# A two-layer decoder trunk on one core: where the dense query and gate products stand among the state updates of the scan stage

## What is computed

```python
proj = h @ p["w_in"]
z, xbc, dt_raw, rg_x, rg_gate, q, k, v, g = split(proj, ...)
y_ssd, ssd_buf_new, ssd_h = _ssd_mixer(z, xbc, dt_raw, ssd_h0, ssd_buf, p)   # the scan
y_ret, ret_h = _retention_mixer(q, k, v, g, pos, ret_h0, p)                  # reads q, k, v, g
mix = concatenate([y_ssd, y_rg, y_ret], -1) @ p["w_out"]

# in the scan, for every sequence with its own kept state S (16 heads x 128 x 64):
y = scores @ v + (q * exp(acum)) @ S       # the kept state is read
S_new = chunk_decay * S + chunk_state      # then scaled and added to
```

## Time and profile before

| | |
|---|---|
| median of 3 runs | 1962.3 us (1961.86 to 1969.98) |
| profiled execution, its own time | 1966.48 us |
| its span | 1964.6 us |
| TensorE matmul busy | 1555.6 us, 79% |
| VectorE busy | 752.6 us, 38% |
| ScalarE busy | 347.8 us, 18% |
| mean DMA rate | 289 GB/s |
| layers | two, the second some 939 us behind the first |

### The profile page before, as it was taken

How to read it: one execution, slowest core, us unless ns; L and a number is a source line. 1 busy time by engine, 2 the same in 40 slices (tenths; PEclk the granted TensorE clock), 3 DMA queues, 4 the chain that set the end, 5 groups by cost and what they waited for, 6 DMA issues and landing times.

```text
span 1964.6 us, 29459 instructions
## 1 busy us (share of the span) xinstructions
PE 1555.6 (79%) x11754; PEld 838.6 (43%) x11754; DVE 752.6 (38%) x1685; ACT 347.8 (18%) x773; POOL 113.6 (6%) x162
## 2 busy tenths in 40 slices
PE   5999988888767767668699998998896776676782
PEld 2764533434433334334266553343353333333441
DVE  0242655667222222122625355466732221122235
ACT  1235311112101111101123531110211111011010
POOL 3000012101000000000020001111000000000000
PEclk8999999988988888889899899998878888788896
DMA  9344335527799999999935443644649999999992
GB/s 332 130 172 176 119 107 178 205 116 286 328 429 428 428 428 429 428 428 427 354 123 195 142 150 96 187 148 180 278 190 428 427 429 429 428 428 429 428 427 85
DMA packets 93463, 567.52 MB, mean 289 GB/s; under 512 B 7062, under 2 KB 7918, under 8 KB 68035
## 3 DMA queue, kind: packets, MB, share of 16 engines
q1 hardware_dynamic: 81666, 532.05, 66.5%
q0 software_dynamic: 11712, 34.32, 6.2%
HBM read 550.53 MB, written 15.81 MB: 288 GB/s over the span
## 4 chain that ended last, share of the span: by engine, by line
PE 45%; DMA 39%; DVE 8%; ACT 2%; issue 2%; DVEq 2%; SPq 1%; PEldq 0%; ACTq 0%; PEld 0%
DMA ring<-in_exp_w_up 36%; PE ps L1453 10%; PE ps L940 8%; PE ps L965 8%; PE ps L1191 3%; PE ps L1316 2%; PE ps L866 2%; DMA ring<-in_w_out 2%; PE ps L947 2%; PE ps L1428 1%; DMA ring<-in_w_ada 1%; PE ps L808 1%; PE ps L1137 1%; PE ps L1161 1%; SPq L604 1%
## 5 line engine op out<-in xcount | busy, mean ns | idle before, releaser
L1453 PE MATMUL ps<-ring,xTb 128*32 128x256 f32 x4224 | 329.1, 480 | 239.9 <-DMA ring<-in_exp_w_up 234.3
L1453 PEld LDWEIGHTS ps<-ring,xTb 128*32 128x32 f32 x4224 | 163.4, 137 | 404.9 <-issue 360.8
L2530 DVE TENSOR_TENSOR hb<-sg,ps 128x128 f32<-128x128 f32 x66 | 25.0, 380 | 493.9 <-ACT sg L1792 493.9
L965 PE MATMUL ps<-ring,hT 128*128 128x512 f32 x384 | 182.7, 630 | 21.4 <-DVE h0s L2106 14.2
L940 PE MATMUL ps<-hT,ring 128*128 128x288 f32 x640 | 165.5, 418 | 5.9 <-ACT hT L1573 2.4
L1428 PE MATMUL ps<-sel,h_tm 128*128 128x128 f32 (+1 forms) x912 | 169.5, 314 | 0.0
L1428 PEld LDWEIGHTS ps<-sel,h_tm 128*128 128x128 f32 x912 | 129.6, 195 | 55.3 <-issue 29.7
L940 PEld LDWEIGHTS ps<-hT,ring 128*128 128x128 f32 x640 | 122.8, 195 | 44.1 <-issue 9.5
L1467 PE MATMUL ps<-ring,hTb 128*32 128x256 f32 x2112 | 130.7, 389 | 5.1 <-DVEq L2533 5.1
L965 PEld LDWEIGHTS ps<-ring,hT 128*128 128x128 f32 x384 | 74.8, 200 | 127.6 <-issue 127.1
L1792 ACT ACTIVATE sg<-ps 128x128 f32<-128x128 f32 x66 | 18.3, 277 | 597.7 <-PE ps L1453 597.7
(11 more groups left out here) (444 smaller groups left out, 1628.3 us busy)
## 6 DMA issues: line engine op xcount, KB each, us to landing
ring<-in_exp_w_gate SPq DMA_DIRECT2D x66, 2048.0 KB, 18.8
ring<-in_exp_w_up SPq DMA_DIRECT2D x66, 2048.0 KB, 23.3
ring<-in_exp_w_down SPq DMA_DIRECT2D x66, 2048.0 KB, 24.8
ring<-in_w_ada SPq DMA_DIRECT2D x24, 2048.0 KB, 11.7
ring<-in_w_in SPq DMA_DIRECT2D x22, 2048.0 KB, 9.0
ring<-in_w_out SPq DMA_DIRECT2D x8, 2048.0 KB, 14.1
h0s<-in_state_ssd POOLq DMA_DIRECT2D x16, 512.0 KB, 7.1
out_ssd_s<-h0s POOLq DMA_DIRECT2D x16, 512.0 KB, 5.4
```

What stands on the lines that cost most here:

```text
L965: last = mm(o[:, :], hT[:, k, T0[i]:T0[i] + P], w[:, k, :], start=(k == 0), stop=(k == KT - 1))
L1453: last = mm(ps[32 * j:32 * j + 32, b, 0:2 * P], xTb[:, k, m * BLK:(m + 1) * BLK], w[:, 0:2, k * D_EXPERT + j * P:k * D_EXPERT + (j + 1) * ...
```

## The change

Both edits are the two sides of one order: the list of PSUM entries (first part) and TensorE's program (second part). No instruction is added or removed; no size changes.

```diff
-HALVES = {-1: (2, 0, 0), 0: (2, 0, 1), 1: (2, 1, 0), 2: (2, 1, 1), 3: (3, 0, 0), 4: (3, 0, 1), 5: (3, 1, 0), 6: (3, 1, 1)}
-FEW = {-1: ((2, "s"),), 3: ((2, 2), (3, "s"))}
+PIECES = {-1: ((2, "s", None), (2, 0, None)), 0: ((2, 1, 0),), 1: ((2, 1, 1),), 2: ((2, 2, None), (3, "s", None), (3, 0, 0)),
+          3: ((3, 0, 1),), 4: ((3, 1, 0),), 5: ((3, 1, 1), (3, 2, None))}
 
 
 def after_state(b):
 
-    few = [(("q", c, j), "A") for c, j in FEW.get(b, ())]
-    c, j, half = HALVES.get(b, (0, 0, 0))
-    last = [(("q", 3, NT - 1), "A")] if b == max(HALVES) else []
-    return few + ([(("q", c, j), "A")] if half else []) + last
+    return [(("q", c, j), "A") for c, j, half in PIECES.get(b, ()) if half != 0]
...
                     def after_state(b):
-                        for c, j in FEW.get(b, ()):
-                            tokens(stream(n0 + c - 2), "q", c, j)
-                            if c == 2 and j == NT - 1:
-                                free_slot(n0)
-                        if b in HALVES:
-                            c, j, half = HALVES[b]
-                            tokens(stream(n0 + c - 2), "q", c, j, range(4 * half, 4 * half + 4))
-                            if b == max(HALVES):
-                                tokens(stream(n0 + 1), "q", 3, NT - 1)
-                                free_slot(n0 + 1)
+                        for c, j, half in PIECES.get(b, ()):
+                            ks = range(KT) if half is None else range(4 * half, 4 * half + 4)
+                            tokens(stream(n0 + c - 2), "q", c, j, ks)
+                            if j == NT - 1:
+                                free_slot(n0 + c - 2)
```

## The result

The changed kernel took 1931.66 us (median of 4 runs, 1929.52 to 1934.92) beside 1962.08 us for the kernel before on the same chip: ratio 0.9839, 95% interval 0.9806 to 0.9872. The profiled execution took 1933.65 us with a span of 1931.8, against 1966.48 and 1964.6. The forecast was 25.1 us less, 1937.2, with a range whose low end was 1933.4 less 2, so 1931.4. So the direction was right and the change was worth more than was forecast: 30.4 us between the medians here, 27.2 in e2.

The account below looks back on a forecast made before the run. In the scan stage TensorE's own work bounds the kernel, with idle waits on VectorE and a lowered clock. Waits and clock recovered, less tail and gap losses, gave 11.6 + 13.5 = 25.1 us: 1962.3 to 1937.2, range 1931.4 to 1945.

Parts of the forecast that it names:

- low end: Whole kernel: no clock loss in the gap before `mix_a`, 1933.4 us, less 2 for scatter of a few runs' median.
- The waits: Scan stage: three TensorE idle times per layer removed, 10.86 us in the first layer and 10.51 in the second.
- The given-back tail: Before `mix_a`: last pair lacks dense work, 8.7 us from reads of state 6 or 7, 2.2 given back per layer.
- third wait: Scan stage, c3 tile 1 waiting for the last half of state 5: 3.31 and 3.30 us removed.
- The clock inside the stage: Dense halves behind the waits, slowed by the low clock: 4.82 us back in the first layer, 6.30 in the second.
- The clock of mix_a: Low clock after the new gap before `mix_a`: 1.9 us lost per layer, bounds nothing and 3.1.
- cold starts in full: Rival: gap before `mix_a` leaves the clock low, the product loses 3.1 us per layer; 1939.6 us, chance 0.14.
- a shift of `mix_a` should reach the end whole: Behind the stage: later work keeps its distance from `mix_a`, so the whole shift of `mix_a` reaches the end.
- No state came late: Rival: last state load 5 us later, VectorE waits at state 7 by 2 to 5 us per layer; chance 0.05.
- lost downstream: Rival: a weight load behind the stage takes half or all of the gain, 1950 to 1962 us; chance 0.07.
- hold on through the mixing: Rival "slower": low clock lasts after the gap; for all 64 `mix_a` prompt matmuls, 1982 us; chance 0.04.

Follow-up runs that it names:

- e2: The changed kernel run again, nothing edited: 1933.82 us (4 runs), ratio 0.9859 to the kernel before.
- e3: Changed kernel with the first wait alone put back (c2 tile 0 in halves, c2 tile 1 whole behind state 1): 1941.46 us, ratio 0.9905.
- e5: Changed kernel with the second wait alone put back (c2 tile 1 in halves behind states 1 and 2): 1944.5 us, ratio 0.9921.
- e6: Changed kernel with the third wait alone put back (c3 tile 1 behind states 5 and 6, j=2 behind state 6): 1933.98 us, ratio 0.9865.
- e1: The kernel before run again, nothing edited: 1962.81 us (12 runs), ratio 1.001.
- e14: The kernel before, nothing edited, third profile: that execution took 1969.16 us.
- e7: Kernel before with three more pairs of dense dummy matmuls (keep_clock(5) instead of 2) ahead of each layer's first gather: 1963.05 us (12 runs).
- e13: Kernel before with one more pair of dummy matmuls (keep_clock(3)) ahead of the first gather: 1958.55 us, ratio 0.9983.
- e4: Changed kernel reordered so that the last dense product is kept for the last pair of states: 1933.25 us (5 runs), ratio 0.9843.
- e8: Changed kernel with three more pairs of dummy matmuls (keep_clock(5)) ahead of the first gather: 1941.56 us (6 runs).

## Why the prediction was right, and where it was short

**The waits: right.** The places in the bank list gave all three waits and their removal, 10.86 and 10.51 us, each shown by putting it back alone (e3, e5, e6). `mix_a` starts 55.5 us behind c2 "s", forecast 55.2.

**The given-back tail: right in size.** From the end of the reads of state 6 to `mix_a` are 8.9 us (forecast 8.7), with the three idle rows behind the last states and 2.35 us from the last state to `mix_a`. e6 shows that it cancels the third wait.

**The clock inside the stage: right on average.** 4.8 and 6.3 us were taken from one profile. They make 11.1; the same halves lost 13.4 us in e1, 13.6 in e14, 10.8 in e7 and 10.7 in e13, 11.9 on average, and each half from 0.04 to 3.1 us, as in the forecast. Against that the changed order always takes 57.3 to 57.4 us from `rep`; the old one took from 68.6 (e7) to 73.1.

**The clock of mix_a: too small.** "I take 1.9 a layer." The changed kernel's first 32 matmuls took 16.99, 16.78, 15.58, 16.69, 17.07 and 16.86 us in three profiles, 2.7 above 14.00 on average, within the bounds of 0 and 3.1. The rival of cold starts in full (3.1) was nearer than the forecast. The Trainium skill ("TensorE: Matmul & The Clock Gate", "What's actually happening"), by which only activity lifts the clock, was the better guide here: the granted clock was 0.50 at the head of `mix_a` in both layers. (Activity is not always enough, though, as the long gathers show.)

By these terms the first two profiles give 22.5 us inside the two stages against 25.1 forecast. The mean of all three profiles of each kernel (169.0 and 144.3 us for both layers) gives 24.7, since e1 and e14 lost more behind the waits than the profile of the forecast. So the sum for the stages was right, in part because two misses offset each other: `mix_a` lost more, and the halves behind the waits had more to give back.

**The step that failed** is the line between the stages and the total: "So a shift of `mix_a` should reach the end whole", together with the low end of the range, "no clock loss in the gap, 1933.4, less 2 for the scatter of a median of few runs". The shift did reach the end. But the sum put everything outside the two stages at nothing. The medians were 30.4 us apart, of which the stages explain 24.7; some 5.7 us came from outside. The profile that the forecast started from held a gather at half clock (14.70 instead of some 8.9 us, and 1.6 us more in the first expert's matmuls behind it). The kernel before meets that in a part of its runs, and the changed kernel did in none of its three profiles. Outside the two stages its three profiles took 1797.4, 1787.2 and 1797.6 us, the changed kernel's 1787.1, 1784.0 and 1790.7: 10 us more with a long gather, nothing with a short one. That the medians differ by more than the stage is worth because of this gather is what the traces suggest; e13, which should have shown it, has an interval that just includes no change. Part of the miss is also the draw of few runs: in e2 the difference was 27.2 us, and the ratio falls inside the range. Two microseconds for scatter were far too few for a kernel whose runs in one sitting lie from 1953 to 1970 us. The forecast could have seen it: the same 48 matmuls had 8.92 us in the trace's first layer and 14.70 in its second.

**Rivals.** No state came late in the changed kernel (it did in e4, by 1.24 us). Nothing was lost downstream. The low clock did not hold on through the mixing: the second half of `mix_a`'s first 32 matmuls ran at full (granted clock 1.00 from 324 to 333 us and from 1252 to 1262).

**Open:** why the order before and that of e4 met the low clock at the second layer's gather in four of five profiles while the changed order did not in three, whether the changed order ever does, and what e8's runs lost beyond its profiled one.

## What to carry to other kernels

When buffers are handed out in a written order, count for each product which entry it waits for; moving one product by one state can take away a wait of 3 to 4 us and the slow matmuls behind it, and the last such move may only carry the gap to the end, where dense work kept back is worth more. Before forecasting from one profile, compare identical groups between repetitions (layers, experts): where they differ by the clock, the total carries that luck, and the range must too. A pair of dense dummy matmuls ahead of a stretch that follows a wait can pay for itself, but their number has to be tried (in the order of e4 one pair gained 8 us and three pairs lost 6 of them again).

## What was not expected of the hardware

A stretch of matmuls can stay at 1.2 GHz although TensorE never rests in it. In the long gathers the engine was busy without a gap, and the granted clock was 0.50 from end to end. Kernel e14, one stretch:

```profile
1431.40:1446.20 14.80, 14.80 (x49) 11.17 (x47) 4.76 (x22) 0.60 (x1) 0.00 (x0) 0.50 0.00 0
```

The same 48 matmuls with one or three more pairs of 512-column matmuls right ahead took 8.3 to 8.4 us, and without them 8.7 to 9.0 where the clock rose soon after they had begun. The halves of 512 columns behind a wait, in contrast, lost 1.4 to 3.1 us in 27 of 30 cases (five profiles of the old order) and nothing to speak of in three, and what followed them ran at its usual pace.
